# Expert rows are weighted as they leave the bank and added in memory onto their token's row by an indirect scatter with addition

## The reference

```python
x = layer_norm(DEEPNORM_ALPHA * x + mix, ln1_g[i], ln1_b[i])
moe = hier_moe(x, ...)
x = layer_norm(DEEPNORM_ALPHA * x + moe, ln2_g[i], ln2_b[i])

def hier_moe(x, ...):
    g_idx = argmax(xt @ w_group + b_group)          # one of 4 groups, weight g_w
    top_vals, top_idx = top_k(logits of the 4 experts of that group, 2)
    top_w = softmax(top_vals) * g_w
    ...
    a = silu(gate) * up * combine[:, :, None]       # combine: top_w at the 2 chosen experts of 16
    y = einsum("tef,efd->td", a, w_down)
```

## Time and profile before

| what | value |
|---|---|
| time, median of 3 runs | 1434.43 us (1432.51 to 1435.21) |
| time of the profiled execution | 1434.39 us |
| its span in the profile | 1432.9 us |
| PE, DVE, ACT, POOL busy | 89%, 56%, 41%, 14% of the span |
| read and written in HBM | 209.90 MB, 33.37 MB |
| mean rate of all transfers | 170 GB/s |

### The profile page before, as it was taken

One profiled execution on the slowest core, in us unless ns is written; L12 is line 12 of the kernel. 1 busy time (PEld: TensorE's weight loads), 2 busy tenths in 40 slices (PEclk: granted clock), 3 DMA queues, 4 the chain that ended last, 5 costly groups with the idle time before them and its releaser, 6 DMA issues.

```text
span 1432.9 us, 21217 instructions
## 1 busy us (share of the span) xinstructions
PE 1278.4 (89%) x8445; PEld 1192.5 (83%) x8445; DVE 808.0 (56%) x1086; ACT 582.6 (41%) x616; POOL 207.5 (14%) x208
## 2 busy tenths in 40 slices
PE   5999999999999999799994297999999889996297
PEld 5999999999999998677883297999998778885297
DVE  4634356453553535778884744355334878885741
ACT  4322222213122123578884522212213488886422
POOL 2300110000000004211212200000004311211300
PEclk9999999999999999799997598999999889998599
DMA  9443334243242231489997421122112479997301
GB/s 313 140 152 122 108 106 137 70 147 106 70 135 77 73 113 45 183 331 412 419 422 272 138 80 43 60 89 89 45 56 96 166 267 423 420 423 282 123 1 66
DMA packets 92547, 244.25 MB, mean 170 GB/s; under 512 B 6070, under 2 KB 53342, under 8 KB 80064
## 3 DMA queue, kind: packets, MB, share of 16 engines
q1 hardware_dynamic: 71520, 170.40, 32.3%
q0 software_dynamic: 16352, 56.12, 11.5%
q10 hardware_dynamic: 4608, 16.78, 2.9%
HBM read 209.90 MB, written 33.37 MB: 170 GB/s over the span
## 4 chain that ended last, share of the span: by engine, by line
PE 76%; DVE 6%; ACT 6%; DMA 5%; issue 4%; POOL 2%; ACTq 0%; SPq 0%; DVEq 0%; POOLq 0%
PE ps L1408 18%; PE ps L1409 18%; PE ps L1410 17%; PE ps L1704 3%; PE ps L1705 3%; PE ps L1706 3%; ACT w_hi L678 2%; PE ps L1503 2%; POOL y_gathered L646 1%; DMA y_scratch<-expert_y 1%; DMA y_gathered<-y_scratch,token_slot 1%; PE ps L1721 1%; PE ps L1723 1%; PE ps L1722 1%; DVE w_lo L944 1%
## 5 line engine op out<-in xcount | busy, mean ns | idle before, releaser
L944 DVE TENSOR_TENSOR w_lo<-w_raw,w_hi 128x2048 fp32r<-128x2048 f32 (+1 forms) x164 | 359.6, 2210 | 123.7 <-ACT w_hi L678 122.5
L678 ACT ACTIVATE w_hi<-w_raw 128x2048 fp32r<-128x2048 f32 (+1 forms) x164 | 300.2, 1847 | 104.7 <-PE ps L1410 75.2
L1408 PE MATMUL ps<-x_hi,w_hi 128*128 128x288 f32 x1024 | 306.5, 299 | 11.5 <-DVE x_lo L1326 11.0
L1410 PE MATMUL ps<-x_hi,w_lo 128*128 128x288 f32 x1024 | 304.7, 298 | 0.0
L1409 PE MATMUL ps<-x_lo,w_hi 128*128 128x288 f32 x1024 | 304.5, 297 | 0.0
L1408 PEld LDWEIGHTS ps<-x_hi,w_hi 128*128 128x128 f32 x1024 | 195.2, 191 | 13.5 <-issue 11.3
L1409 PEld LDWEIGHTS ps<-x_lo,w_hi 128*128 128x128 f32 x1024 | 195.2, 191 | 0.0
L1410 PEld LDWEIGHTS ps<-x_hi,w_lo 128*128 128x128 f32 x1024 | 195.0, 190 | 0.0
L1408 PE MATMUL ps<-w_hi,x_hi 128*128 128x256 f32 x480 | 137.5, 286 | 4.0 <-DVE v_stage L984 4.0
L1409 PE MATMUL ps<-w_lo,x_hi 128*128 128x256 f32 x480 | 136.9, 285 | 0.0
L1410 PE MATMUL ps<-w_hi,x_lo 128*128 128x256 f32 x480 | 136.9, 285 | 0.0
(11 more groups left out here) (263 smaller groups left out, 2141.0 us busy)
## 6 DMA issues: line engine op xcount, KB each, us to landing
w_raw<-in_moe_w_gate_up SPq DMA_DIRECT2D x64, 1024.0 KB, 7.9
w_raw<-in_moe_w_down SPq DMA_DIRECT2D x32, 1024.0 KB, 9.4
w_raw<-in_a_w_in SPq DMA_DIRECT2D x24, 1024.0 KB, 5.3
y_scratch<-expert_y ACTq DMA_DIRECT2D x32, 512.0 KB, 8.1
w_raw<-in_a_w_out SPq DMA_DIRECT2D x12, 1024.0 KB, 5.1
w_raw<-in_b_w_in SPq DMA_DIRECT2D x12, 1024.0 KB, 5.2
w_raw<-in_ple_w_gate SPq DMA_DIRECT2D x8, 1024.0 KB, 8.2
v_scratch<-v_stage POOLq DMA_DIRECT2D x12, 512.0 KB, 3.5
```

The source lines that it names most:

```text
L678: act.activation(whi[:, j, 0:n], raw[:, j, 0:n], ACT.Copy).then_inc(hi_done, 1)
L944: dve.tensor_tensor(wlo[:, j, 0:n], raw[:, j, 0:n], whi[:, j, 0:n].bitcast(f32), ALU.subtract).then_inc(split_done, 1)
L1408: pe.matmul(out, sh, mh, start=first, stop=False)
L1410: ins = pe.matmul(out, sl, mh, start=False, stop=final)
```

## The change

The second normalisation no longer collects rows. A new array in memory, `sum_dram`, has a row for each of the 576 tokens and 128 rows for empty slots. POOL writes into it first the rows of `x_tok`, which now are already multiplied by ALPHA (POOL scales `ln_params` by ALPHA once for that; the activation and the weights divide it out again). These are three stores behind the fourth gather. ACT's `y_out` multiplies by a slot's weight `slot_w` while copying, and POOL's `scatter` adds the 128 rows of `expert_y` onto the rows that `row_idx` names; an empty slot has weight 0 and a row of its own behind the tokens. Each scatter waits for the one before, and `y_out` still waits for `y_st`, which is now the scatter's. In the gathers empty slots carry a number beyond the last row and are left out, where they fetched row 0 before. When the last scatter has landed, SP loads the five blocks from `sum_dram`, and DVE and ACT work on them as they are. ACT's scaling of `x_tok` is gone, and DVE computes the places of rows only in the branch for more than 128 rows. New on PE are 20 small products that place the weights (`slot_weights`), new on DVE three operations that prepare them.

```diff
+    sum_dram = [nc.dram_tensor(f"sum_scratch{l}", (T + CAP, D), f32).ap() for l in range(DEPTH)]
...
@@ sync, behind the loads of ple_w_gate
+                sp.wait_ge(eu_used, EU * (l + 1))
+                sp.wait_ge(etl_ok, 2 * NE * (l + 1))
+                sp.wait_ge(y_st, 16 * NE * (l + 1))
+                for i in range(NT):
+                    if i >= 4:
+                        sp.wait_ge(nz_ok, 2 * NT * l + NT + i - 3)
+                    sp.dma_start(yrows(i, tok(i), 0), sum_dram[l][P * i:P * i + tok(i), :]).then_inc(yg_ld[i % 4], 16)
@@ gpsimd
                 pool.wait_ge(ln_ld, 32 * (l + 1))
+                pool.tensor_scalar(lnp[:, :, :], lnp[:, :, :], ALPHA, None, ALU.mult).then_inc(ln_ok, 1)
...
                     pool.indirect_dma_start(out=xg[:, s % 2, :], out_offset=None, in_=x_dram[l][:, :],
-                                            in_offset=bass.IndirectOffsetOnAxis(ap=idx[:, s:s + 1], axis=0)).then_inc(xg_ld[s % 2], 16)
-
-                for s in range(NE):
+                                            in_offset=bass.IndirectOffsetOnAxis(ap=idx[:, s:s + 1], axis=0),
+                                            bounds_check=T - 1, oob_is_err=False).then_inc(xg_ld[s % 2], 16)
+
+                def scatter(s, sem_):
+                    pool.indirect_dma_start(out=sum_dram[l][:, :], out_offset=bass.IndirectOffsetOnAxis(ap=row_idx[:, s:s + 1], axis=0),
+                                            in_=y_sb[:, :], in_offset=None, compute_op=ALU.add).then_inc(sem_, 16)
+
+                def expert_rows(s):
+                    pool.wait_ge(y_cp, NE * l + s + 1)
+                    if l or s:
+                        pool.wait_ge(y_st, 16 * (NE * l + s))
+                    scatter(s, y_st)
+
+                for s in range(4):
                     gather(s)
...
+                pool.dma_start(sum_dram[l][0:TP, :].rearrange("(i p) d -> p i d", p=P), xtok[:, 0:4, :]).then_inc(a_st, 16)
+                pool.dma_start(sum_dram[l][TP:T, :], xtok[0:TS, 4, :]).then_inc(a_st, 16)
+                pool.dma_start(sum_dram[l][T:T + CAP, :], xtok[:, 0, :]).then_inc(a_st, 16)
+                pool.wait_ge(row_ok, l + 1)
+                pool.wait_ge(a_st, 48 * (l + 1))
+                for s in range(4, NE):
+                    gather(s)
+                    expert_rows(s - 4)
+                for s in range(NE - 4, NE):
+                    expert_rows(s)
...
-                    for i in range(NT):
-                        if i >= 4:
-                            pool.wait_ge(st_ok, 2 * NT * l + NT + i - 3)
-                        for k in range(2):
-                            pool.indirect_dma_start(out=yrows(i, tok(i), k), out_offset=None, in_=y_dram[l][0:rows, :],
@@ scalar
-                    act.activation(y_sb[:, :].rearrange("p (b t) -> p b t", b=2), ps[:, 4:6, :], ACT.Copy).then_inc(y_cp, 1)
-                    act.wait_ge(y_cp, q + 1)
-                    act.dma_start(y_dram[l][ds(it * (P * step) + P * s, P), :], y_sb[:, :]).then_inc(y_st, 16)
+                    act.wait_ge(wslot_ok, l + 1)
+                    act.activation(y_sb[:, :].rearrange("p (b t) -> p b t", b=2), ps[:, 4:6, :], ACT.Copy,
+                                   scale=slot_w[:, ds(it * step + s, 1)]).then_inc(y_cp, 1)
...
-                act.wait_ge(x_st, 16 * NT * (l + 1))
-                act.activation(xtok[:, 0:4, :], xtok[:, 0:4, :], ACT.Copy, scale=ALPHA)
-                act.activation(xtok[0:TS, 4, :], xtok[0:TS, 4, :], ACT.Copy, scale=ALPHA).then_inc(xs_ok, 1)
@@ vector, behind the experts
-                        for k in range(0 if i < 3 else 1, 2):
-                            ch.link(dve.scalar_tensor_tensor(out=xtok[0:t, i, :], in0=yrows(i, t, k), scalar=wtop[0:t, k, i:i + 1],
-                                                             in1=xtok[0:t, i, :], op0=ALU.mult, op1=ALU.add))
                         for h in range(2):
-                            ins = dve.bn_stats(vstat[0:t, i, h, :], xtok[0:t, i, 512 * h:512 * h + 512])
+                            ins = dve.bn_stats(vstat[0:t, i, h, :], yg[0:t, i % 4, 0, 512 * h:512 * h + 512])
@@ tensor
+                def slot_weights():
+                    pe.wait_ge(wsel_ok, l + 1)
+                    out = ps[:, 7, 256:384].rearrange("p (a e) -> p a e", e=NE)
+                    for k in range(2):
+                        for i in range(NT):
+                            for h in range(2):
+                                ins = pe.matmul(out, amat[:, k, i, :], wsel[:, k, i, h, :].unsqueeze(1).to_broadcast([P, 8, NE]),
...
                     if s < NE - 1:
                         turn_slots(s + 1, it, step, (s + 1) % 2)
+                    if s == 0:
+                        slot_weights()
```

163 lines of the change are left out of this document (91 added, 72 removed).

## The result

The change makes the kernel slower: 1463.88 us, median of 4 runs (1461.98 to 1469.35), against 1434.82 us for the kernel before beside it. The ratio is 1.0206, with an interval of 1.018 to 1.0232. The forecast was 1442 with a range of 1402 to 1485. The sign and the range held, and the likeliest case of 1435 to 1466 too, but +29 us is four times the forecast +7. That the time lies inside the likeliest case is in part luck, as the part on the prediction shows.

A forecast was written before the change was run, and what follows sets the result against it. DMA engines and PE nearly tie as bounds of an expert step; with the change the copy-scatter ring decides. Layers sum to +1.9 and +5.2, together +7.1 on 1434.4, so 1442 us, range 1402 to 1485.

The forecast's parts named there:

- the likeliest case: Whole kernel: a ring of 11.1 to 12.4 us a step gives 1435 to 1466 us; chance 0.47.
- start of the experts: Before expert 1's copy: scatter 0 waits for the sum rows' stores, landing near 625; loss 2.1 us a layer.
- twelve steps: Copy of expert 1 to copy 13: step grows from 9.99 to 11.4 us, 16.9 us lost a layer.
- last two experts: Copy of expert 13 to copy 15: 17.8 us instead of 15.9, landings 9.0 and 6.0; loss 1.9 a layer.
- behind the last copy: Last scatter, five plain loads, normalising until x^T: 26.0 us against 45.0 and 41.7; gain 19.0 and 15.7.
- The ring: Each expert step: expert_y copy, POOL's wake, scatter's landing of 10.0 us, semaphore, then next copy; period 11.4 us.
- sign of this failure: Start of the experts: forecast would be wrong if the first steps stood 7 us or more for the sum rows.
- the engines' 10.9 us: Each expert step: DMA work of weights 7.57, gather 0.74 and scatter 2.6 us, less than the ring's period.
- rival 2: Expert steps: the engines' 10.9 us binds and not the ring; 1429 us; chance 0.15.
- POOL's scaling of ln_params: Ahead of POOL's first product, while it waits for PE's turn of block 0; costed at nothing.
- Rival 1: Expert steps: addition nearly free and landing early; 1397 us, or 1417 with a ring of 10.4; chance 0.22.
- Rival 3: Expert steps: scatter lands late at 13, ring 14.4; 1522 us; chance 0.16 including what lies between.

The follow-up runs named there:

- e1: Changed kernel with each block's token rows stored to sum_dram right behind its x_dram store, padding rows ahead of the first gather; 1449.35 us, ratio 1.0077.
- e3: Changed kernel with a second expert_y buffer, so ACT's copy waits for the scatter before the last; scatters still wait for one another; 1458.77 us.
- e9: e2 with two expert_y buffers and two sums, odd experts' sum not added, so no scatter waits for the one just before; 1441.26 us.
- e4: Changed kernel with the same scatter but without addition, rows overwriting each other, so the output is wrong; 1431.93 us, ratio 0.9969.
- e13: Changed kernel redesigned: plain bounded scatter to a row per choice, two expert_y buffers, two loads and two additions a block at the end; 1418.73 us.
- e2: Changed kernel with a bound on the scatter, so empty slots are left out and their padding rows are not stored; 1458.19 us, ratio 1.0154.
- e7: Kernel before the change, with only the change's bound on its gathers, so empty slots are left out; 1435.21 us, ratio 1.0004.
- e14: e13 with POOL adding the token rows of blocks 1 to 4; 1415.06 us, ratio 0.9863 against the kernel before the change.

## Why the prediction was right in sign and short in size

Forecast and measured, both layers, in us (the measured ones from the profiles, whose spans differ by 31.3):

| term | forecast | measured |
|---|---|---|
| start of the experts | +4.2 | +25.6 |
| twelve steps | +33.8 | +31.6 |
| last two experts | +3.8 | +7.8 |
| behind the last copy | -34.7 | -32.4 |
| elsewhere | 0 | -1.3 |

**The likeliest case was hit in part by luck.** The prediction drew 1435 to 1466 for rings of 11.1 to 12.4 us. The ring came out at 11.28, and with that its own sum gives 2 * (2.1 + 15.5 + 1.9) - 34.7 = +4.3 us, 1439. Most of the other 25 us came from terms that it had mis-sized, the start above all.

**The term that was mis-sized is the start.** The step read: the stores' "2.88 MB, 6.9 us of the engines" beside the weights "land near 625", scatter 0 "goes at about 628". The last one landed at 634.1 and it went at 637.0, and that is 9 us of the error in layer 0. The work was priced somewhat low (POOL's queue took 0.433 * 22 = 9.5 us of the engines, for 3.16 MB with gathers in them). The larger fault is the rate: 11 us for 6.9 us of work is 0.63 of the engines, and no row said so. The earlier trace rows has 0.61 busy, which leaves 0.39, and at that rate the stores would take 17.7 us; POOL waited 18.20. But that they agree is chance, for the engines were not shared in this way. The slices above show POOL's queue with all the engines first and with 2.6% of them last. The 2 MB store landed at 625.5, just as I had forecast for all three. The scatter waited for the last and smallest share of the work, which moved beside a full stream of weights. Why the last 0.04 MB took four microseconds no view shows. The Trainium skill (DMA: Bandwidth & Descriptors, Queues, rings and completion order) says that an engine serves the queues that have work for it in turn, packet by packet. This trace agrees only in part: between 622 and 626 us the two queues have 51.7% and 48.2%, but in the four microseconds before it is 102.6% and 0.5%. My own text had named the sign of this failure, first steps that stand 7 us or more for the sum rows. e1, which moves the stores and nothing else, gives 17.5 us back. A smaller part of the term came from believing expert 0's rows were ready 1 us earlier: copy 0 came 0.8 us earlier in layer 0, about as forecast, but the scatter behind the fifth gather could not use it.

**The steps came out as forecast, with a mean landing of 9.5 and 9.9 where I took 10.0**, period 11.28 against 11.4, copies that idle 1.3 to 3.9 us in layer 0 (up to 5.3 in layer 1) and gathers with fewer bytes. The chain shows this ring and no other. What I had wrong is what stands next to it. I held the engines' 10.9 us as a bound below the ring, and rival 2 as what would come if the ring were quick. The engines were busy all of the step, e3 shortened the ring and the landings grew by about as much, and e9 took the ring away and found 11.53. The scatter costs 2.9 us of the engines (2.6 taken), and a load of weights costs 2.6 beside it (2.52 taken) and 3.0 in e9. A sum of fixed prices for each transfer does not foresee that.

**The last two experts** lost 7.8 where 3.8 was forecast. I had let their landings fall to 9.0 and 6.0, since the weights run out. In the chain of layer 0 the one before the last took 6.96 us and the last 6.42. In e4 this cut is 31.4 us, as in the kernel before: the loss is all the addition's.

**Behind the last copy** the sum was good to 2.3 us of 34.7. Its parts were further off than their sum. From the end of copy 15 to the scaling of x^T it is 27.0 us in layer 0, where I had 26.0. The wake was right (0.27, 0.3 taken). The scatter took 6.42 (6.0 taken), SP's issues 0.9 (0.4), and the loads, issued together, 6.18 (2.9 taken, from the landing of a store that runs alone), together 4.2 us too little. Against that I had 3.3 us from the landing to the first normalising and 10.0 for four blocks. The chain has 1.8 and 8.3, for it runs through the second load and so over three blocks: 3.2 us too much.

**POOL's scaling of ln_params** was costed at nothing behind PE's turn. It took 5.4 us a layer (532.51 to 537.9), and POOL's first product still waited for PE behind it, 3.12 us in layer 0 and 0.68 in layer 1. The cost is not to be seen in the last column of the table.

Rival 1 (addition nearly free) is out, e4 being what it would have needed. Rival 3 (landings of 13 throughout, a step of 14.4) did not come. But its sign, landings of 12 and more, is in layer 1, four times among experts 1 to 12 (12.2 to 13.2 us); each has one of some 8 us behind it, and the mean stays at 9.9.

## What to carry to other kernels

An addition in the DMA engines is not a store that saves a later pass: here it cost the engines twice a plain scatter, brought an order in which each scatter waits for the landing of the one before, and wanted an array filled beforehand. Giving each contribution a row of its own with a plain scatter, and adding on a compute engine at the end, kept nearly half of the gain (15 of 32 us behind the last copy) with none of the costs in the cuts before it, and made the kernel 1.1% faster than before instead of 2.1% slower. When transfers are put beside a full stream, ask who waits for the last of them, and do not take its landing from the bytes: here the first 2 MB landed as forecast and the last 0.5 MB nine microseconds later; the same stores cost 17.5 us more behind the fourth gather than beside the stores of x_dram.

## What the runs showed of the hardware

- An indirect scatter with addition of 128 rows of 4 KB took 2.9 us of the 16 engines, without addition 1.4; alone it landed in 6.42 us, without addition in 3.32 (e4), and with the empty slots left out as well in 3.23 (e13).
- Rows beyond the bound are left out but remain packets, 289 a step as against 290, now under 512 bytes. In the scatter with addition they saved nothing in the steps (11.4 us against 11.28), while 64 rows fewer, not issued at all, saved 1.03 us a step.
- A scatter with a bound was issued 0.8 us behind the end of its copy, one without 0.27 us (e2 and the changed kernel).
- In e9 the weights' loads in the chain of 652 to 728 us land in 10.4 to 12.5 us beside scatters with addition, in e13 (690 to 728 us) in 8.55 to 9.66 beside plain ones, with about as many rows a step and the engines at 0.97 and 0.98. In the changed kernel, whose weights do not bind, they land in 8.4 and 8.7 us (medians in 670 to 760 us). Why they are late in e9 (the memory, the engines' own reading and writing, or the order of both) is not settled: no run here tells these apart.
- Three stores on POOL's queue and a stream of weights on SP's shared the engines unevenly: in 618 to 622 us POOL's queue had 102.6% of them and SP's 0.5%, with a load of SP issued at 618.03, and in 630 to 634 us it was 2.6% and 98.3%.
- Leaving 44% of the rows out of a gather at a DMA share of 1.01 changed neither the share nor the step (e7).
- An addition on VectorE of 128 x 1024 values took 3.29 instead of 1.23 us once while POOL added as well (e14); another, at whose start POOL began to add, took 1.23.
